# Raw residual routing, whole rows of 4 KB in gather and scatter, spread slots, and an output product by column halves in a hybrid decoder layer

## The reference, cut to what matters

```python
    x = x + jnp.einsum('blm,md->bld', y, lw['w_out'])
    x = x + moe_ffn(rmsnorm(x, lw['norm_ffn_g']), lw['router_group_w'], lw['router_group_b'],
                    lw['router_expert_w'], lw['router_expert_b'], lw['exp_w_gu'], lw['exp_w_down'])
...
def moe_ffn(x, wg_r, bg_r, we_r, be_r, w_gu, w_down):
    lg = xt @ wg_r + bg_r                       # 4 groups
    pg = softmax(lg); gsel = argmax(lg)
    le = xt @ we_r + be_r                       # 32 experts, 8 in a group
    tv, ti = top_k(le of the chosen group, 2)
    gate = pg[gsel] * softmax(tv)
    # every row goes through its two experts, weighted by gate:
    # (silu(x @ w_gu[e][:, :512]) * (x @ w_gu[e][:, 512:])) @ w_down[e]
```

## Time and profile before

| what | value |
|---|---|
| time, median of 3 runs | 896.74 us (896.69 to 897.82) |
| the profiled execution: its own time | 897.07 us |
| its span from first to last instruction | 895.3 us |
| PE busy | 745.3 us (83%) |
| DVE, ACT, POOL busy | 217.6, 137.9, 186.9 us |
| DMA | 247.55 MB, mean 276 GB/s |
| hardware queue q1 | 232.00 MB, 65.5% of 16 engines' span |
| mean granted TensorE clock | 0.962 of full |

### The profile page before, as it was taken

One profiled execution on the slowest core, in us unless ns is written; L12 is line 12 of the kernel. 1 busy time (PEld: TensorE's weight loads), 2 busy tenths in 40 slices (PEclk: granted clock), 3 DMA queues, 4 the chain that ended last, 5 costly groups with the idle time before them and its releaser, 6 DMA issues.

```text
span 895.3 us, 10055 instructions
## 1 busy us (share of the span) xinstructions
PE 745.3 (83%) x3636; PEld 384.8 (43%) x3636; DVE 217.6 (24%) x546; ACT 137.9 (15%) x338; POOL 186.9 (21%) x186
## 2 busy tenths in 40 slices
PE   3999999979898999829999997777777777787783
PEld 3788688857666545613333332222222222222220
DVE  4331104267759322171011110010010010100110
ACT  4212313013253401100000000000000000000000
POOL 6010000150300000011322331322312313223121
PEclk9999999989897999859999999999999999999997
DMA  9642823010510294458999999999999999999981
GB/s 309 127 135 60 262 103 102 4 69 1 207 77 1 83 423 181 164 225 339 413 410 408 408 406 415 415 408 417 409 412 414 410 413 416 408 416 409 413 341 30
DMA packets 75812, 247.55 MB, mean 276 GB/s; under 512 B 24796, under 2 KB 44139, under 8 KB 51163
## 3 DMA queue, kind: packets, MB, share of 16 engines
q1 hardware_dynamic: 62625, 232.00, 65.5%
q0 software_dynamic: 11776, 8.58, 4.4%
q10 hardware_dynamic: 1378, 6.54, 1.8%
HBM read 240.99 MB, written 24.92 MB: 297 GB/s over the span
## 4 chain that ended last, share of the span: by engine, by line
PE 39%; SPq 33%; DVE 11%; DMA 11%; issue 3%; ACT 2%; POOL 0%; ACTq 0%; DVEq 0%; POOLq 0%
PE bank L1063 36%; SPq L570 23%; SPq L577 9%; DMA reg_b<-in_exp_w_gu 6%; PE bank L1066 3%; DMA reg_a<-in_exp_w_gu 3%; DMA reg_x<-in_x_prompt 1%; DVE reg_a L1722 1%; DVE reg_a L1802 1%; DVE reg_y L1973 1%; DVE reg_a L1712 1%; DVE reg_x L1712 0%; DVE small L1763 0%; POOL small L673 0%; DVE reg_a L1714 0%
## 5 line engine op out<-in xcount | busy, mean ns | idle before, releaser
L1063 PE MATMUL bank<-reg_w,reg_y 128*64 128x512 f32 (+2 forms) x512 | 136.9, 585 | 19.3 <-DMA reg_w<-in_exp_w_gu 19.3
L1063 PE MATMUL bank<-reg_b,reg_y 128*64 128x512 f32 x528 | 124.3, 601 | 25.8 <-DMA reg_b<-in_exp_w_gu 18.0
L1063 PE MATMUL bank<-reg_a,reg_y 128*64 128x512 f32 x528 | 124.5, 607 | 24.0 <-DMA reg_a<-in_exp_w_gu 17.8
L1977 DVE TENSOR_TENSOR reg_y<-reg_y,bank 128x256 f32<-128x256 f32 x32 | 13.5, 421 | 426.5 <-ACT reg_y L1046 426.5
L1063 PEld LDWEIGHTS bank<-reg_w,reg_y 128*64 128x64 f32 (+2 forms) x512 | 46.1, 146 | 104.5 <-issue 59.6
L1063 PE MATMUL bank<-reg_b,reg_w 128*128 128x260 f32 x384 | 85.3, 383 | 0.0
L1063 PEld LDWEIGHTS bank<-reg_b,reg_y 128*64 128x64 f32 x528 | 34.1, 136 | 106.8 <-issue 56.5
L1063 PEld LDWEIGHTS bank<-reg_a,reg_y 128*64 128x64 f32 x528 | 34.5, 138 | 105.3 <-issue 50.6
L1063 PEld LDWEIGHTS bank<-reg_b,reg_w 128*128 128x128 f32 x384 | 72.7, 190 | 12.0 <-issue 1.1
L673 POOL TENSOR_TENSOR small<-small 128x1 f32<-128x1 f32 (+4 forms) x18 | 20.2, 1125 | 198.1 <-DVE small L1855 68.1
L739 POOL DMA_INDIRECT out_y_p<-reg_y,reg_q x16 | 25.3, 1581 | 170.6 <-ACT reg_y L1050 170.6
(11 more groups left out here) (341 smaller groups left out, 656.9 us busy)
## 6 DMA issues: line engine op xcount, KB each, us to landing
reg_a<-in_exp_w_gu SPq DMA_DIRECT2D x44, 1024.0 KB, 28.1
reg_b<-in_exp_w_gu SPq DMA_DIRECT2D x44, 1024.0 KB, 28.3
reg_w<-in_exp_w_gu SPq DMA_DIRECT2D x40, 1024.0 KB, 28.2
reg_a<-in_exp_w_down SPq DMA_DIRECT2D x22, 1024.0 KB, 28.5
reg_b<-in_exp_w_down SPq DMA_DIRECT2D x22, 1024.0 KB, 28.6
reg_h<-in_exp_w_down SPq DMA_DIRECT2D x20, 1024.0 KB, 28.8
reg_w<-in_w_in SPq DMA_DIRECT2D x9, 1024.0 KB, 10.7
reg_w<-in_w_out SPq DMA_DIRECT2D x1, 4096.0 KB, 13.2
```

Source lines behind the costliest of these rows:

```text
L1063: return eng.matmul(out, lhsT, rhs, start=start, stop=stop, skip_group_check=True)
L1977: tt(hid[b], silu[b], bank[2 + b][:, 256:512], ALU.mult).then_inc(S["hid_made"], 1)
```

## The change

- The router works on the raw residual. The gain of the norm is multiplied into the router weights (on POOL) and, for the experts, into the turned rows (`copy_xe`, which becomes a multiply). rstd is multiplied in behind the products: into the logits, into the argument of Silu, and into the output scale of each slot. So two scales a slot are tabled instead of one, and `h2` and `second_norm` are gone; `ffn_in` holds `x1`.
- Gather and scatter move whole rows of 4 KB: 64 indices instead of 128. Buffer b of the gathered rows and of `y_out` lies in partitions 64b to 64b+63. ACT writes a result in two copies of 64 x 512.
- Spread slots: slot 4i+j holds position i+16j.
- The output product runs over the first column halves of all tiles and then over the second halves; turnings and routing products stand between chunks of a half. `w_out` is loaded in two halves.
- The choice runs in two groups of tiles, n = 0 to 2 and n = 3, 4. The rows are counted with the sample tile first.
- Expert 2's loads: down weights first, then gate and up chunks 0, 1 after `Y3.0` and 2, 3 after `Y3.1`.

The diff, cut to its core:

```diff
-            eng.iota(cap_iota, pattern=[[0, 2], [1, CAP]], base=0, ...)
+            eng.iota(cap_iota, pattern=[[0, 2], [1, 16], [16, 4]], base=0, ...)
...
+            eng.wait_ge(S["rows_stored"], 16 * 4)
+            eng.wait_ge(bank_full[bank_of["NT3"]], turn_of["NT3"] + 1)
+            load_down(2, 2)
+            eng.wait_ge(bank_full[bank_of["Y3.0"]], turn_of["Y3.0"] + 1)
+            load_gu(2, 2, parts=(0, 1))
             eng.wait_ge(bank_full[bank_of["Y3.1"]], turn_of["Y3.1"] + 1)
-            load_gu(2, 2)
-            eng.wait_ge(S["h2_stored"], 16 * NTILE)
-            eng.wait_ge(bank_full[bank_of["hTb3"]], turn_of["hTb3"] + 1)
-            load_down(2, 2)
+            load_gu(2, 2, parts=(2, 3))
...
+            eng.tensor_tensor(rt_w, rt_w, params[:, P_FFN_G:P_FFN_G + 8].unsqueeze(2).to_broadcast([128, KC, 36]), ALU.mult).then_inc(S["rtw_scaled"], 1)
...
             def gather(e):
-                idx = bass.IndirectOffsetOnAxis(ap=row_of[:, e:e + 1], axis=0)
-                eng.indirect_dma_start(xe_rows[e % 2], None, h2_halves, idx, bounds_check=2 * T - 1, oob_is_err=False).then_inc(x_gathered[e % 2], 16)
+                at = slice(CAP * (e % 2), CAP * (e % 2) + CAP)
+                idx = bass.IndirectOffsetOnAxis(ap=row_of[0:CAP, e:e + 1], axis=0)
+                eng.indirect_dma_start(xe_rows[at], None, x1_dram, idx, bounds_check=T - 1, oob_is_err=False).then_inc(x_gathered[e % 2], 16)
...
+                    idx = bass.IndirectOffsetOnAxis(ap=row_of[0:CAP, at:at + 1], axis=0)
...
-                eng.activation(silu[b], bank[2 + b][:, 0:256], ACT.Silu).then_inc(S["silu_done"], 1)
+                eng.activation(silu[b], bank[2 + b][:, 0:256], ACT.Silu, scale=slot_scale[:, 1, bass.ds(e, 1)]).then_inc(S["silu_done"], 1)
...
-                eng.activation(y_out[b], bank[6 + b][:, :], ACT.Copy, scale=slot_gate[:, bass.ds(e, 1)]).then_inc(S["y_copied"], 1)
+                for s in range(2):
+                    at = slice(CAP * s, CAP * s + CAP)
+                    ins = eng.activation(y_out[b][:, 512 * s:512 * s + 512], bank[6 + b][at, :], ACT.Copy, scale=slot_scale[at, 0, bass.ds(e, 1)])
+                ins.then_inc(S["y_copied"], 1)
...
+            for n in range(1, NTILE):
+                drained(eng, f"NT{TILES[n]}")
+                project_out(n, 0, {6: (turn_x1, (0, 0)), 7: (turn_x1, (0, 1))} if n == 1 else {3: (route, (0,))} if n == 2 else {})
+            project_out(1, 1, {4: (turn_x1, (1, 0))})
+            for n in range(2, NTILE):
+                project_out(n, 1, {2: (turn_x1, (n - 1, 1)), 5: (route, (n - 1,)), 7: (turn_x1, (n, 0))})
...
+            eng.wait_ge(S["mask_made"], 1)
+            positions("posA", range(3))
+            turn_x1(4, 1)
             route(4)
+            eng.wait_ge(S["mask_made"], 2)
+            positions("posB", [3, 4])
...
-                for j in range(4):
-                    ins = turn(bank[1][:, 128 * j:128 * j + 128], xe_rows[b][:, 128 * j:128 * j + 128])
+                at = slice(CAP * b, CAP * b + CAP)
+                by_channel = xe_rows[at, :].rearrange("n (p c) -> n c p", c=KC)
+                for c in range(KC):
+                    ins = eng.transpose(bank[1][:, CAP * c:CAP * c + CAP], by_channel[:, c, :], ident[at, at])
...
+            early, late = range(3), range(3, 5)
+            group_choice(early)
+            add_half(3, 1)
+            expert_choice(early)
+            ask_rstd(3)
+            add_half(4, 1)
+            count_before(early, "posA")
+            ask_rstd(4)
+            find_slots(pk, early)
+            group_choice(late)
+            expert_choice(late)
+            count_before(late, "posB")
...
+            eng.tensor_copy(pk_next, pk)
+            link(tt(gate, gate, rstd[:, 0:5].unsqueeze(2).to_broadcast([128, 5, 2]), ALU.mult))
+            for which in range(2):
                 for k in range(2):
-                    ins = eng.tensor_copy(ids[:, k, :, 2 + piece], ohp[:, k])
+                    factor = gate[:, :, k] if which == 0 else rstd[:, 0:5]
+                    ins = tt(ohp[:, :, k, :], oh[:, :, k, :], factor.unsqueeze(2).to_broadcast([128, 5, N_EXP]), ALU.mult)
                 link(ins)
+                for piece in range(3):
+                    out = scale_ids[:, :, :, 3 * which + piece, :]
+                    ins = eng.tensor_copy(out, ohp)
...
+                    if piece < 2:
+                        link(tt(ohp, ohp, out, ALU.subtract))
...
-                eng.tensor_copy(xe[b], bank[1][:, :].rearrange("p (j s n) -> p j s n", j=4, s=2)).then_inc(S["xe_made"], 1)
+                tt(xe[b], bank[1][:, :].rearrange("p (c n) -> p c n", c=KC), gain_x.unsqueeze(2).to_broadcast([128, KC, CAP]), ALU.mult).then_inc(S["xe_made"], 1)
```

More of the change, by code:

```diff
@@ L153, in psum_jobs @@
         take(f"NT{i}")
-    last = None
     take("L", 7)
-    for i in TILES:
-        take(f"Y{i}.0")
[L158 to L166, removed]
+    first, *others = TILES
+    take(f"Y{first}.0")
+    take(f"Y{others[0]}.0")
+    take(f"hTa{first}")
+    take(f"hTb{first}")
+    for i in others[1:]:
+        take(f"Y{i}.0")
+    take(f"Y{others[0]}.1")
+    take(f"hTa{others[0]}")
+    for last, i in zip(others, others[1:]):
+        take(f"Y{i}.1")
+        take(f"hTb{last}")
+        take(f"hTa{i}")
+    take("posA")
+    take(f"hTb{others[-1]}")
+    take("posB")
     take("cnt", 6)
@@ L336, in layer_kernel @@
-        flr = rt(8)
-        cnt = rt(8)
+        y_pair = reg_h.t[:, 4096:5120]
+        y_out = [y_pair[CAP * b:CAP * b + CAP, :] for b in range(2)]
+        scale_ids = reg_q.cut(960).bitcast(BF16).rearrange("p (t k f e) -> p t k f e", t=5, k=2, f=6)
+        slot_v = reg_y.cut(64, "p (x e) -> p x e", x=2)
+        slot_no = reg_y.cut(32)
+        row_of = reg_y.cut(64).bitcast(U32)
+        row_next = reg_y.cut(64).bitcast(U32)
+        slot_scale = small.cut(2 * N_EXP, "p (x e) -> p x e", x=2)
@@ L338, in layer_kernel @@
+        lg8, mx8, mi8, tv8 = [reg_y.cut(40, "p (t e) -> p t e", t=5) for _ in range(4)]
+        reg_w.rewind(8192)
+        ti8 = reg_w.cut(40, "p (t e) -> p t e", t=5)
+        gate = reg_w.cut(10, "p (t k) -> p t k", t=5)
+        psel = reg_w.cut(5)
+        pk_next = reg_w.cut(10, "p (t k) -> p t k", t=5)
         mask_bf = sb("mask_bf", [128, 5, N_EXP], BF16)
@@ L351, in layer_kernel @@
         thr = small.cut(8)
-        valid = small.cut(5)
+        valid = small.cut(1)
         minus_half = small.cut(160)
@@ L369, in layer_kernel @@
         sumsq = small.cut(8)
+        x1_sq = small.cut(10, "p (t h) -> p t h", t=5)
+        gain_x = small.cut(8)
         rstd = small.cut(8)
@@ L561, in _, with load_gu @@
             eng.dma_start(x1[:, 0:4, :], x_dram).then_inc(S["x_reloaded"], 16)
-            def load_gu(e, g, free=None):
+            def load_gu(e, g, free=None, parts=range(GU_PARTS)):
                 width = KC // GU_PARTS
-                for part in range(GU_PARTS):
+                for part in parts:
                     lo = part * width
@@ new lines, in route, with project_out @@
+                ins.then_inc(S["routed"], 1)
+            def project_out(n, half, between_chunks):
+                i = TILES[n]
+                r = ROWS[i]
+                ps = claim(eng, f"Y{i}.{half}")
+                for c in range(KC):
+                    if c in between_chunks:
+                        step, args = between_chunks[c]
+                        step(*args)
+                    ins = mm(ps[0:r, :], yT[:, c, COL[i]:COL[i] + r], w_out[half][:, c, :], c == 0, c == KC - 1)
+                filled(ins, f"Y{i}.{half}")
@@ L1993, in _ @@
                 eng.wait_ge(S["next_at"], r + 1)
[L1994 to L1995 removed]
+                find_slots(pk_next, range(NTILE))
+                rows_of_slots(row_next, r + 2, 4 * r + 4)
                 expert(n + N_EXP - 1, 1, True)
```

428 lines of the change are left out of this document (204 added, 224 removed).

## The result

The kernel after takes 925.22 us (median of 4 runs, 924.78 to 926.48) against 897.28 for the kernel before on the same chip: 1.0313 times, interval 1.0296 to 1.0331. It is slower by 28 us where 883.5 was forecast. The profiled execution has a span of 923.2 us.

A forecast was written before the change was run, and what follows sets the result against it. The expert loop is bound by DMA transfers: expert 3's load start, the slowest engine's time, and the tail. Terms -5.4 (start), -7.8 (stream) and 0 (tail) sum to -13.2 us, median 883.5; range 879 to 888, 8 in 10 875 to 891.

The forecast's parts named there:

- Up to expert 0: Start of the expert loop: +4.0 us to the last add, -9.4 from there, so expert 0 starts 5.4 us earlier.
- the interleaved products: Output projection: an extra routing product, half turnings and switches delay the last add by 4.0 us, to 373.8.
- Rival B: Start of expert 0 does not move, only the stream gains: 889 us; chance 0.09.
- One count on the way to the map: Kernel before's gathers and adds: blocks of eight neighbouring partitions would leave eight equal engines last, a share of 0.5.
- The stream: Expert loop transfers: -7.8 us, from -5.3 for a lighter heaviest engine and -2.5 for fewer empty slots.
- If four neighbouring slots belong to one engine, the sixteen engines get 77, ...: 64-slot gathers and adds: heaviest engine has 77 whole rows, 154 halves instead of 176, worth -5.3 us.
- The map of 128 partitions: Kernel before's gathers and adds: an engine serves four neighbouring partitions and four 32 further on; two engines have 176 half-rows.
- rival A: End of the weight stream: the two late engines are slow of themselves, not by their rows: 889 us; chance 0.10.
- the empty slots of the adds: Expert loop, empty slots of gathers and adds: heaviest engine's empties fall from 416 to 230, worth -2.5 us.
- Rival D: Stream: adding a 4 KB row costs as little as its bytes, -17.6 instead of -5.3 us, 871; chance 0.05.
- Rival C: Stream: 64 rows always spread over the same eight engines, heaviest 140 rows, +17 us, 914; chance 0.07.
- The tail: After the last expert: second result copy +0.7 us, cheaper scatter issues (1.2 for 1.55) -0.7, sum 0.

The follow-up runs named there:

- the first experiment: Kernel before with only the slot order changed, row position p going to engine p mod 8 of each half: 888.87 us, ratio 0.9903.
- The even order: Kernel after with positions k, 31-k, 32+k and 63-k on engine k, still 64 whole rows: 900.24 us, ratio 1.0029.
- the plain one: Kernel after with its 64 whole rows in plain slot order instead of spread: 911.09 us, ratio 1.0153.
- half rows in the order of eight groups: Kernel after with 2 KB half rows in 128 partitions, positions dealt out over eight engines of each half: 883.81 us, ratio 0.984.
- the first of the table: Kernel after with balanced slots, 4 KB rows gathered in 128 slots, one half skipped, and 2 KB half-row adds: 884.5 us, ratio 0.9852.
- the gather in two: Kernel after with half rows throughout, balanced slots, and the gather cut into two 64-partition transfers: 903.68 us, ratio 1.0067.

## Why the prediction was wrong

**Up to expert 0: right.** Last add 372.60 (forecast 373.8, from 369.79), so the interleaved products cost +2.8 where +4.0 was taken. From there to expert 0: 21.1 us (forecast 21.9). Step by step: to the routing product 2.2 (2.5), the product 2.0 (2.3), to the mask 3.8 (3.3), to the indices 4.3 (4.5), the tables 7.0 (7.25), gate table and start 1.8 (2.0). Start 7.4 us earlier instead of 5.4, inside the bounds given. Rival B fell.

One count on the way to the map was off and changed nothing: blocks of eight neighbours would give the engines of a half 256, 256, 251 and 191 half-rows, so four or six engines last in all, not eight. Two last speaks against them all the same.

**The stream: wrong, and the step is named by the sentence "If four neighbouring slots belong to one engine, the sixteen engines get 77, ..."** and its term of -7.8 us. Its parts, each measured:

1. The map of 128 partitions was right (rival A, slow engines, fell with the first experiment), but it was carried over to a transfer of 64, which no row of before shows. There the runs fit engines that serve pairs of slots, and the spread order, even by fours, is the worst by pairs: 125 rows on the heaviest instead of 77. The even order takes the stream from 505.6 to 482.2: 23.4 us for 56 rows, 0.42 each. Plain to even is 9.4 us for 20 rows, 0.47 each. The 0.48 us of the prediction was near; the count was wrong. Not all of the 23.4 is eight engines left over at the end: by 860 us the kernel after is already behind by 4.8 MB (158.7 against 163.5 MB, some 12.7 us at the even order's rate), at the same share. There 195 of its weight packets take over 700 ns, against 2 in the even order and 7 in the plain one. So at 125 rows part of the loss shows as longer packets and not as idle engines; what those packets wait for, the trace does not say.
2. The 64-slot gather slows the weights. From 482.2 to 465.3: 16.9 us, for which the prediction had no term. Its half-row counterpart, two transfers of 64 against one of 128, gives 488.0 - 470.0 = 18.0.
3. What is left is what the prediction described: the even order with a gather whose engines keep their partitions, 465.3 against 475.6 before, -10.3 where -7.8 was forecast (the heaviest engine is lighter than the 77 rows assumed: 69 rows of adds, 74 of gather by the two maps). In it the empty slots of the adds are worth 467.5 - 465.3 = 2.2 and, with the half-row gather, 470.0 - 467.4 = 2.6; forecast 2.5. Rival D, an addition as cheap as its bytes, fell with the same pairs: no 12 us more are in it.

-10.3 + 16.9 + 23.4 = +30.0, the stream's loss.

Rival C had the right sign and a near time (914) with a chance of 0.07. Its mechanism, always the same eight engines with 140 rows at most, was not it: with eight engines in groups of four, plain slots would have been the slowest. But eight engines did end up with nearly all rows, by the order of slots. The chance was set too low on an argument the prediction itself weakened: all that it had for a 64-partition transfer was the map of 128. The first bursts of a gather, where the loads rest, would show it in one run.

What remains argued is why the 64-slot gather slows the weights. The theory 'foreign partitions' says: in 128 slots each engine writes its rows to the same partitions as its weights, and in 64 slots sixteen engines share what eight served, and write rows where other engines' weights go. The first experiment shows the map for rows in 128 slots; that the weights go by the same map, no run here shows. The runs fit: the loss comes back with either row size whenever 64 slots are dealt out, and goes when they are not; the adds, which read SBUF, cost nothing. But doubling the rows in one half changed nothing, so no single half of SBUF is the limit over the whole loop; a theory of blocked partitions must lie within one burst, where all rows go to one half in both kernels. This was not tried further.

The Trainium skill (SBUF — State Buffer, "Door 1: The DMA port swizzle") says that partitions 0 to 63 reach only eight of sixteen DMA ports, and that 64 partitions are hardly faster than 32. That rate was not measured here, and the count of ports does not tell the runs apart: the rows of one gather go to one half of the partitions in both kernels, and the one with 64 slots slows the loads beside it by 17 us over the loop, the one with 128 slots does not. The page draws no line between loads and stores; here the adds from 64 partitions cost the stream nothing.

**The tail: +5.3 instead of 0.** The 0.7 for the second copy was right; the cheaper issues (1.39 for 1.55, not 1.2) gave 0.3 back. 1.6 us are the down product at the lower clock, for which the prediction had no term. It is not a matter of whole rows: of the kernels tried here four took 5.35 us for the last down product (half rows in the order of eight groups, 64 whole rows in plain slots, half-row gather with whole-row adds, and the first of the table) and eight took 3.65; why the clock fell in those is not shown. Some 0.5 is the last add's landing, and 2.8 us lie between DVE's last copy and the end of the span. The last copy in the kernel with half-row adds and even slots (span 881.7):

```profile
876.11 0.20 DVE L2062 COPY reg_y<-reg_y 128x64 uint32<-128x64 uint32 x1 [10.28 <-POOLq L772]
```

and with whole rows and the 128-slot gather (span 882.5):

```profile
867.15 1.37 ACT L1077 ACTIVATE reg_h<-bank,small 64x512 f32<-64x512 f32 x2 [5.40 <-PE bank L1091]
...
874.21 0.21 DVE L2065 COPY reg_y<-reg_y 128x96 uint32<-128x96 uint32 x1 [10.91 <-POOLq L774]
```

To the end of the span it is 5.5 us in the one and 8.3 in the other, though the work ends 1.9 us earlier in the latter. All kernels with whole-row adds show 8.3, those with half-row adds 5.3 or 5.5, but for the gather in two with 7.3. In the instruction records one instruction fills it, POOL's closing DRAIN: 7.91 us with whole-row adds, 5.14 before and in most with half-row adds, 4.85 in the one with whole-row gather in 64 slots and half-row adds, 6.85 in the gather in two. The last packet of the adds has landed by then, so it does not wait for them; why it takes longer stays open. With the second copy and a start that is 2.1 us later in this trace, it takes back what the emptier adds gain in the stream: half rows and whole rows end at the same time, 883.55 and 883.62.

## What to carry to other kernels

Before a gather or scatter changes its number of partitions, find out again which engine serves which slot: spread a known number of rows, look at an undisturbed burst, and balance the heavy slots by that map; one line of slot order, even by the right map, took 8 us off the kernel before; one that was even by the wrong map added 14 us to plain slots. When the DMA share is 1.0 and GB/s falls, the cause can be another queue's small transfer: divide share by packets and compare. Beside a saturated weight stream try the gather in the 128-partition shape of the weights, even with half of its slots empty; here it was worth 16.9 us of stream.

## What was unexpected of the hardware

- The software transfers of 64 partitions here fit a deal in pairs (slots 2k, 2k+1, 2k+32, 2k+33 to engine k): 925.2, 911.1 and 900.2 us for 125, 89 and 69 rows on the heaviest engine, and 40 and 10 packets at once in the first gather of the first two.
- Such a gather makes other engines' weight packets longer (0.288 against 0.277 us in the mean) and its own too (196 against 159 ns), 16.9 us in all; such an add costs the stream nothing.
- A gather of 128 slots with half of them out of bounds costs no time that shows (465.3 us of stream, the best of all).
- Kernels with whole-row adds end some 2.8 us of span later behind the last work than those with half-row adds: POOL's closing DRAIN takes 7.91 instead of 5.14 us, for no reason that the trace shows.
